# One transformer layer's expert stage: a new order behind the page loop, and slot sums as two whole products

## The reference

```
h = rmsnorm(x);  proj = h @ w_in
ya = Mamba-2 branch                       # ends in @ w_ssm_proj
yb = latent attention, ends in @ w_mla_proj   # samples read 16 pages of 128 cached positions each
x  = x + (sigmoid(gate_a)*ya + sigmoid(gate_b)*yb) @ w_out
h  = rmsnorm(x)                           # PEER, for each token t and each of 8 heads
q  = h @ wq                               # 8 heads x 256
s1, s2 = q[:128] . keys1, q[128:] . keys2 # 128 keys each
top 16 of s1, top 16 of s2, top 16 of the 16x16 sums -> 16 experts idx, softmax weights g
x  = x + sum_k g_k * gelu(u[idx_k] . h) * v[idx_k]
```

## Time and profile before

| | us |
|---|---|
| median of 3 runs | 2219.43 |
| lowest, highest | 2215.1, 2222.27 |
| the profiled execution | 2226.05 |
| its span, first to last instruction | 2224.5 |
| PE, DVE, ACT, POOL busy | 1727.0, 1486.0, 460.4, 662.6 |
| mean granted clock of PE | 0.824 |
| data moved by DMA | 743.71 MB, 334 GB/s |

### The profile page before, as it was taken

One profiled execution on the slowest core, in us unless ns is written; L12 is line 12 of the kernel. 1 busy time (PEld: TensorE's weight loads), 2 busy tenths in 40 slices (PEclk: granted clock), 3 DMA queues, 4 the chain that ended last, 5 costly groups with the idle time before them and its releaser, 6 DMA issues. The chain is left out here.

```text
span 2224.5 us, 30923 instructions
## 1 busy us (share of the span) xinstructions
PE 1727.0 (78%) x11202; PEld 890.5 (40%) x11202; DVE 1486.0 (67%) x3801; ACT 460.4 (21%) x1382; POOL 662.6 (30%) x598
## 2 busy tenths in 40 slices
PE   6999989887787666666689998888777866666665
PEld 5887657632243111110168876575323321111110
DVE  3555433777887887878736554438787788787785
ACT  2334211112112111111122532102211211111111
POOL 0001000245445444444300000003444544444441
PEclk9999999978789676676889999999877875667667
DMA  5447498799999999999754476968999999999995
GB/s 194 155 138 277 145 349 290 284 385 417 419 421 420 421 407 421 418 412 407 318 171 161 123 270 216 343 243 338 421 421 410 421 420 405 416 421 415 412 410 239
DMA packets 188212, 743.71 MB, mean 334 GB/s; under 512 B 16339, under 2 KB 76172, under 8 KB 117634
## 3 DMA queue, kind: packets, MB, share of 16 engines
q0 software_dynamic: 83296, 582.18, 64.2%
q1 hardware_dynamic: 104754, 159.46, 21.0%
HBM read 730.32 MB, written 11.46 MB: 333 GB/s over the span
## 5 line engine op out<-in xcount | busy, mean ns | idle before, releaser
L1152 PE MATMUL ps<-arena 64*64 64x512 f32 x4096 | 757.5, 837 | 388.6 <-DVE arena L1735 380.3
L2286 POOL DMA_INDIRECT arena<-in_peer_uv,arena x528 | 623.5, 1181 | 821.9 <-PE ps L1152 647.9
L1726 DVE CUSTOM_DVE_ANT_0 arena<-arena,h 128x1024 f32<-128x1024 f32 x512 | 627.4, 1225 | 216.7 <-DMA arena<-in_peer_uv,arena 205.2
L1152 PEld LDWEIGHTS ps<-arena 64*64 64x64 f32 x4096 | 139.2, 165 | 955.0 <-DVE arena L1735 896.7
L505 PE MATMUL ps<-ht_tok,wring 128*128 128x264 f32 (+2 forms) x1664 | 369.9, 379 | 7.5 <-DMA wring<-in_w_in 7.1
L505 PEld LDWEIGHTS ps<-ht_tok,wring 128*128 128x128 f32 x1664 | 298.5, 194 | 78.0 <-issue 18.9
L2062 ACT ACTIVATE arena<-arena 128x1 f32<-128x1 f32 x528 | 105.7, 203 | 1011.2 <-DVE arena L1726 1004.1
L1735 DVE TENSOR_SCALAR arena<-consts,arena 128x64 f32<-128x64 f32 (+1 forms) x528 | 164.5, 311 | 19.7 <-ACT arena L2062 19.4
L514 PE MATMUL ps<-consts,h 128*128 128x128 f32 (+2 forms) x174 | 39.3, 334 | 50.8 <-DVE h L1255 27.4
L2267 POOL DMA_DIRECT2D nrow<-in_norm_ffn x2 | 1.1, 536 | 209.6 <-PE ps L514 209.6
L505 PE MATMUL ps<-arena,wring 128*128 128x264 f32 x256 | 61.3, 393 | 0.0
(11 more groups left out here) (333 smaller groups left out, 1846.8 us busy)
## 6 DMA issues: line engine op xcount, KB each, us to landing
arena<-in_pages SPq DMA_DIRECT2D x256, 272.0 KB, 4.7
wring<-in_w_in SPq DMA_DIRECT2D x38, 1024.0 KB, 6.0
arena<-in_peer_uv,arena POOLq DMA_INDIRECT x528
h<-in_state_ssm POOLq DMA_DIRECT2D x16, 512.0 KB, 5.6
out<-h POOLq DMA_DIRECT2D x16, 512.0 KB, 4.7
wring<-in_w_ssm_proj SPq DMA_DIRECT2D x8, 1024.0 KB, 9.5
arena<-in_w_out SPq DMA_DIRECT2D x8, 1024.0 KB, 14.7
wring<-in_peer_wq SPq DMA_DIRECT2D x8, 1024.0 KB, 6.5
```

The lines of the kernel that those rows point to most:

```text
L1152: last = pe.matmul(ps[to:to + 64, SUM_BANK[t] + i, :], diag[rows, n % DIAGS, 0:64], ring[rows, HOME[n % RING], cols], start=n in TILE_FIRS ...
L1726: dve.tensor_tensor_reduce(ring[:, HOME[k], 0:D_MODEL], ring[:, HOME[k], 0:D_MODEL], tokens, 1.0, 0.0, ALU.mult, ALU.add, dots[:, column(n ...
L2286: pool.indirect_dma_start(ring[:, HOME[k], :], None, table, bass.IndirectOffsetOnAxis(ap=idx[:, TOPK * u + j:TOPK * u + j + 1], axis=0)).t ...
```

## The change

1. **The page loop takes the prompt's mla pieces**, all 256 prompt columns at once. `PROMPT_PIECES` and `PROMPT_LATER` are dealt out anew: ssm pieces mostly in the later place, and mla in halves 12 to 15. SP loads the mla blocks at i = 11 and 13.
2. **Behind the loop** PE goes straight to `out(k, 0)`, then `out(0, 1)`, turns of rows, queries and scores of head 0, and only then the samples: mix, heads (in `wide` banks, emptied by ACT), and their mla as `sample_mla_parts` (column-tiled over 512 columns) and `sample_mla` (summing by `sel8`). `out(1, 1)`, `out(2, 1)`, `out_samples`, `out(3, 1)` stand between and behind.
3. **`best_experts`** handles both halves in one pass over 512 columns and writes the index at once; its first run is no longer woven with gated products.
4. **Places and waits**: `HOME` puts slot 3 in place 7; w_out's blocks lie in places 3 to 6; slots 3, 4, 6 and 7 wait for heads, sums and `out(3, 1)`. `late_tiles` moves most additions one slot later.
5. **The sum of a slot** is two products over all 128 partitions with a 128 x 128 diagonal (over `ident`), in place of four quarters; `tile_sum` has two additions of 128 partitions in place of four of 64.

```diff
-HOME = (0, 1, 7, 2, 3, 4, 5, 6)
+HOME = (0, 1, 2, 7, 3, 4, 5, 6)
...
+    0: [("scores", (0, 0))], 1: [("scores", (0, 1))], 4: [("turns", (0, 0, 0)), ("turns", (0, 0, 1))],
+    5: [("values", (0,))], 6: [("scores", (1, 1))], 7: [("ssm", (5,))], 9: [("turns", (1, 0, 0)), ("turns", (1, 0, 1))],
+    10: [("ssm", (7,))], 11: [("values", (1,))], 12: [("mla", (0,)), ("mla", (1,))], 13: [("mla", (3,))], 14: [("mla", (4,)), ("mla", (5,))], 15: [("mla", (7,))],
 }
 PROMPT_LATER = {
+    1: [("ssm", (0,))], 2: [("ssm", (1,))], 3: [("ssm", (2,))], 4: [("ssm", (3,))], 5: [("scores", (1, 0))], 6: [("ssm", (4,))],
+    8: [("ssm", (6,))], 9: [("turns", (1, 1, 0)), ("turns", (1, 1, 1))], 12: [("mla", (2,))], 14: [("mla", (6,))],
 }
...
+                    def sample_mla_parts():
+                        pe.wait_ge(sem("wide_free"), 4 + marks["heads", 2])
+                        first = DC * TOKENS + 24 + SEQ
+                        for half in range(2):
+                            w = state["mla", 4 * half]
+                            b = wide.fill()
+                            for c in range(4):
+                                last = pe.matmul(ps[32 * c:32 * c + 32, b, :], shared[:, first + c * TOKENS:first + c * TOKENS + 32], w[:, c, :],
+                                                 start=True, stop=True, skip_group_check=True)
...
                         for half in range(2):
-                            if t < 2:
-                                for i in range(2):
-                                    rows, to = slice(64 * i, 64 * i + 64), 64 * ((i + half) % 2)
-                                    last = pe.matmul(ps[to:to + 64, SUM_BANK[t] + i, :], diag[rows, n % DIAGS, 0:64], ring[rows, HOME[n % RING], cols],
-                                                     start=n in TILE_FIRST, stop=n in TILE_LAST, skip_group_check=True)
-                                continue
+                            last = pe.matmul(ps[0:outs, SUM_BANK[t] + half, :], diag[:, n % DIAGS, 0:outs],
+                                             ring[:, HOME[n % RING], D_MODEL + half * 512:D_MODEL + (half + 1) * 512],
+                                             start=n in TILE_FIRST, stop=n in TILE_LAST, skip_group_check=True)
...
+                        picks = hot[0:r, :].rearrange("p (i j) -> p i j", j=TOPK)
+                        then(dve.tensor_tensor(picks, bc(sel[0:r, :], 2, TOPK), bc(cst("iota")[0:r, :], 1, 2 * TOPK), ALU.is_equal))
...
-                        table, outs = (cst("eye64"), 64) if SLOT[n][0] != SAMPLE_UNIT else (cst("mod8"), SAMPLES)
+                        table, outs = (ident, P) if SLOT[n][0] != SAMPLE_UNIT else (cst("mod8"), SAMPLES)
...
-                        if n == 2:
-                            pool.wait_ge(sem("aux_full"), marks["heads", 1])
-                        elif n in (3, 5, 6):
-                            pool.wait_ge(sem("aux_full"), marks["out", n // 2, 1])
+                        if n == 3:
+                            pool.wait_ge(sem("wide_full"), marks["heads", 2])
+                        elif n == 4:
+                            pool.wait_ge(sem("aux_full"), marks["sums", 0])
+                        elif n == 6:
+                            pool.wait_ge(sem("aux_full"), marks["sums", 1])
+                        elif n == 7:
+                            pool.wait_ge(sem("aux_full"), marks["out", 3, 1])
```

More of the change, by code:

```diff
@@ L919, in half_scores, with sample_mla @@
+                    def sample_mla():
+                        pe.wait_ge(sem("wide_free"), 4 + marks["mla_parts"])
+                        b = aux.fill()
+                        for m in range(DC):
+                            last = pe.matmul(ps[:, b, m * SAMPLES:(m + 1) * SAMPLES], mla_parts[:, m * P:(m + 1) * P], cst("sel8"), start=True, stop=True)
+                        aux.filled(last)
+                        marks["late_mla"] = aux.n
                     def half_scores(i):
@@ new lines, in best_experts @@
+                        yield
+                        for rows, first, count in ((slice(0, r), 0, TOPK),) if t < 2 else ((slice(0, 64), 0, TOPK // 2), (slice(64, P), TOPK // 2, TOPK // 2)):
+                            last = dve.scalar_tensor_tensor(out=idx[rows, TOPK * u:TOPK * u + count], in0=sel[rows, first:first + count], scalar=float(N_KEYS),
+                                                            in1=sel[rows, TOPK + first:TOPK + first + count], op0=ALU.mult, op1=ALU.add)
+                        last.then_inc(sem("idx_ready"), 1)
@@ L1759, in _ @@
+                            last = dve.tensor_tensor(x[0:r, t, half * 512:(half + 1) * 512], x[0:r, t, half * 512:(half + 1) * 512],
+                                                     ps[0:r, SUM_BANK[t] + half, :], ALU.add)
+                        last.then_inc(sem("tile_added"), 1)
+                    for _ in best_experts(0):
                         pass
-                    out(0, 1)
+                    out(1, 1)
                     ahead = best_experts(1)
-                    for half in range(2):
-                        for _ in range(3 - half):
-                            next(ahead)
-                        copy4(hp[2][:, half * 512:(half + 1) * 512])
@@ L1767, in late_tiles @@
                     def late_tiles(n):
-                        if n < 3:
-                            out(n + 1, 1)
+                        if n == 0:
+                            sample_gated()
+                        elif n == 1:
+                            out(2, 1)
+                        elif n == 2:
+                            for half in range(2):
+                                copy4(hp[2][:, half * 512:(half + 1) * 512])
                         elif n == 3:
+                            out(3, 1)
+                        elif n == 4:
```

215 lines of the change are left out of this document (99 added, 116 removed).

## The result

The kernel after takes 2233.8 us (median of five runs, 2224.3 to 2234.2) where the kernel before took 2218.8 in the runs beside it: a ratio of 1.0059, with an interval of 1.0034 to 1.0084. A second comparison on another occasion gave 1.0056 (1.0039 to 1.0073). So by the ratios the change makes the kernel slower by 12 to 13 us (the plain medians lie 15.0 and 10.6 us apart), where 13 us of gain were forecast. Single executions of one kernel differ by up to 10 us either way (2208.7 to 2228.7 in 35 runs of the kernel before), and the profiled one of before lay above its median, so the two profiles differ by less: the spans are 2224.5 and 2232.2 us, +7.7. What follows on single traces explains those 7.7 us; what a part of the change is worth is read from medians.

The account below looks back on a forecast made before the run. The DMA at 421 GB/s was taken as the bound, with gains only in its holes: -4.5 - 0.5 - 7.3 - 0.8 = -13.1 us, so 2219.4 - 13.1 = 2206.3 us, range 2192 to 2226.

Parts of the forecast that it names:

- The bound: Gather stages: a full DMA at 421 GB/s bounds the kernel, 2.49 us per slot; its holes together are 27 us.
- Whole products, their price: Slot sums on PE: 1.75 us a slot at the high clock, weight loads hidden, mean price +0.26 us of PE.
- Inside the 15 us of slack: nothing on the path: Gather stage: PE's +0.26 us per slot stays within the ring's 15 us of DMA work in flight and costs nothing.
- My list for a unit: PE in a 16-slot unit with queries: slots, queries and scores take 36.0 of 39.8 us, leaving 3.8 us.
- The first rival: Units with queries: PE becomes the bound through paid weight loads or a low clock; 2240 us, chance 0.12.
- Slot 8 waits for the x of all tiles, about 438. With 14 MB given out by then the DMA is just fed: Early gather stretch: slot 8 goes out at about 438 with the DMA still fed; 3.7 us of holes per layer.
- Choosing experts: `best_experts`: first chain 9.1 us, 4.5 us shorter; 17 steps in place of 24 take back 7.3 of 14.6 us later holes.
- The page loop: Halves 2 to 15, with the mla pieces moved in: about 103 us, +7 (bounds +3 and +13.7).
- From the loop to the first gather: Page loop to slot 0: 7 - 7.5 - 7.9 = -8.4 us, first gather at about 408.
- The start is worth nothing, within 3 us per layer: First gather: the earlier start gains nothing, since both orders have the same bytes left for the DMA at about 411.
- the -5.0: Early holes of the gather stages: gain of 4.5 us in the first layer and 0.5 us in the second.
- The second rival: Early holes stay, slots 4 to 8 come later than listed, the loop grows by 10 or more; 2218 us, chance 0.17.

Follow-up runs that it names:

- the mixed kernel: Kernel after with early sums of x, quarters in slots 0 to 127, whole products in 128 to 255, queries unmoved: 2206.4 us, ratio 0.9959 to the kernel before.
- added wait: Kernel after with early sums of x and quarters, first gather held until the second head's queries of tile 0 are made: 2213.7 us, ratio 0.9986 to the kernel before.
- Without the two causes: Kernel after with DVE's late additions for x taken off the slots' landings and quarters in place of whole products: 2209.0 us, ratio 0.9966 to the kernel before.
- the run with the old choosing: Kernel after with early sums of x and quarters, choosing experts in 24 steps as in the kernel before: 2221.4 us, ratio 1.0020 to the kernel before.
- all three settings: Quarters against whole products, ratios to the kernel before: old order 1 and 1.0036; new order, late x 1.0015 and 1.0056, 1.0059; new order, early x 0.9966 and 1.0000.

## Why the prediction was wrong

**The bound.** Right: the DMA at 421 GB/s, and the time is made or lost in its holes.

**Whole products, their price.** Right in each number of its own. Eight slots back to back take 13.92 us, 1.74 each and 1.72 from one to the next; 1.75 was forecast. The clock stands at 0.97 to 1.00 in the gather stage but for its first slots; the diagonal takes 0.344 us, 0.35 was forecast. The weight loads are hidden: the 32 passes of eight slots take 0.435 us each, with a load of 0.19 us for each. By the rule of the Trainium skill (TensorE: Matmul & The Clock Gate, Part 3, The mechanism), that a load overlaps only with products in other row groups, they would be paid; the measurement decides against it for these products, and agrees with the background buffer of the same page (Part 2, Step-by-step).

**"Inside the 15 us of slack: nothing on the path".** This is the step that failed first, worth 7.5 to 10 us. I took the ring as full and the unit as an average one. The slack was real from slot 40 on: there the traces with whole products are no longer than those without (565.3 and 564.4 us to the last slot against 566.0 and 567.1), and in the second tile whole products cost nothing that can be measured (the mixed kernel, 0.9959). In the first 40 slots of each layer the ring has just run empty, PE has to fill it, and every microsecond of a slot counts. My list for a unit (36.0 of 39.8 us) also left out the rows of unit 0, 3.7 us: with them it is 39.7 of 39.8, and with the low clock of the first slots beyond it. The first rival had the sign, with a larger size (2240, that is +21 us), for a reason that was wrong: it let PE become the bound through weight loads or a low clock, and it got 0.12 because the rows spoke against both. That the measured time lies near it is luck: PE becomes the bound with its loads hidden and its clock high.

**"Slot 8 waits for the x of all tiles, about 438. With 14 MB given out by then the DMA is just fed".** This is the step that failed second, worth 11 to 13 us. The time of x was right (438.8; 437.65 in the kernel before). But slot 8 needs slot 0's sum behind it, which took 4.1 us at a low clock, and slot 9 another 2.75: 442.94 and 445.69. Fourteen MB from 406.3 on last to 406.3 + 14 x 2.49 = 441.2 us at the full rate, so that there was no reserve, where I should have asked for eight slots' time to refill. And I set 438 beside the 439.11 of the kernel before as if it were equal, though this order starts 10 us earlier: counted from slot 0, x had become later by as much as the start was earlier. The holes of this early stretch were 12.1 us in the first layer and 10.9 in the second for the two places named above, and 3.7 each were forecast.

**Choosing experts.** The chain was right: 396.87 to 405.97, 9.1 us as forecast. The step "that is where the 14.6 us of later holes come from; I take back half, 7.3" was wrong: the later stretches give 13.7 us of holes by the table above, where the earlier trace rows gave 14.6. What the shorter choosing saves in the new order is 12 us by the ratios; the trace shows 7 of them, and they lie in units 1 and 2, while the ring is being filled. In the old order it saves nothing that was measured, so that the term was the wrong one in place and in size.

**The page loop.** Right: 103.1 us for halves 2 to 15, 103 forecast, against 95.8.

**From the loop to the first gather.** Right within 2 us in this trace, 406.33 where 408 was forecast; the other traces of this order with the new choosing and no added wait lie between 400.9 and 405.9, 2 to 7 us ahead of the forecast. The three weight loads did not stand as one block from 403 to 411: two were given out at 398.95 and 399.48, the third at 408.36, and from 405.0 to 408.4 the DMA moved 104 GB/s. "The start is worth nothing, within 3 us per layer" isn't borne out: 4.7 us of delay cost 2.2 us per layer, and the same share of the 8.4 us that were forecast would be some 4 us (an estimate).

**Behind the slots.** tile_sum takes 1.28 us, 1.4 forecast, and the time behind the last gather is 2.4 us shorter.

**The sum.** Without the two causes the new order is worth -7.5 us (0.9966) where -13.1 was forecast: 5.6 us fall to the smaller terms. No run divides them, and parts 1, 2 and 4 of the change were not tested one by one, but for the late additions; the run with the old choosing (1.0020) says that what is left of the gain hangs on part 3. Whole products (0 in the sum, +7.5 to +10 measured) and the late x (a part of the -5.0, +11 to +13 measured) make the other 20 us between forecast and result. The second rival named the place ("slots 4 to 8 come later than in my list") but priced it as a gain missed, not as a loss; slots 4 to 7 even came earlier than in my list (420.6 to 425.9), and slot 8 later.

## What to carry to other kernels

Slack in a ring of buffers is a stock and can be used up: before an edit is priced at nothing because a queue stands ahead, look for the stretch in which that queue is being filled, and add up the engine's work there with everything that is in it once. Where a wait moves, compare it with the work given out until then, in the bounding resource's own time, and leave as much reserve as refilling needs. Keep additions that another engine waits for out of a program order in which each stands behind the landing of one more transfer; here other transfers shared the DMA, and the landings came 5 us apart in place of 2.5.

## What the runs showed of the hardware

The eight instructions of a slot's quarters took 1.09 us at the high clock. Whole-product passes with a 128 x 128 load each stood 0.43 us apart, 1.72 us a slot, so the quarters are the faster form by 0.63 us although they load weights twice as often. A clock that was low after 8.8 us of waiting cost 2.9 us in the next eight slots of whole products (16.84 against 13.92; 2.0 in a second trace), which ten useless products prevented, with no gain in the median. The mean granted clock of the kernel is 0.98 with whole products and 0.82 with quarters, and in all three settings the twin with the lower clock is the faster one: here the mean clock did not tell which kernel is faster.
